# Decoder layer with product-key experts: the transposes of a key tile spread among the products of the tile before

## What is computed

```python
q = (ht @ w_q).reshape(t, PEER_HEADS, 2, PEER_HALF)
sc = jnp.einsum("thcd,hckd->thck", q, subkeys)
s1, i1 = lax.top_k(sc[:, :, 0], PEER_TOPK); s2, i2 = lax.top_k(sc[:, :, 1], PEER_TOPK)
...
experts = (e1 * PEER_N_KEYS + e2).reshape(t, PEER_HEADS * PEER_TOPK)
ug = jnp.take(u, eb, axis=0); vg = jnp.take(v, eb, axis=0)
act = jax.nn.gelu(jnp.einsum("tkd,td->tk", ug, hb)) * gb
return jnp.einsum("tk,tkd->td", act, vg)
```

## Time and profile before

| | |
|---|---|
| runs | 2933.47, 2937.51, 2937.99 us; median 2937.51 us |
| profiled execution | 2933.1 us, span of its instructions 2931.0 us |
| granted TensorE clock, mean | 0.995 |
| share of the span busy | TensorE matmuls 98%, weight loads 87%, VectorE 82%, GpSimd 57%, ScalarE 36% |
| the sweep | about 855 to 2183 us of the span |

### The profile page before, as it was taken

The page is one execution under the profiler, slowest core; times in us unless marked ns, Lnnn a source line. Parts: engine busy times, 40 slices in busy tenths (PEclk is TensorE's granted clock), DMA queues, the critical chain, the costliest instruction groups (busy, mean ns, idle before and its releaser), DMA issues.

```text
span 2931.0 us, 40438 instructions
## 1 busy us (share of the span) xinstructions
PE 2879.4 (98%) x14769; PEld 2546.0 (87%) x14769; DVE 2392.2 (82%) x3106; ACT 1057.1 (36%) x1375; POOL 1672.4 (57%) x1078
## 2 busy tenths in 40 slices
PE   7999999999999999999999999999999999999999
PEld 6888777778899999999999999999997777877787
DVE  6555888855679898988989898899777998999898
ACT  4121433341334343434333343444233333333333
POOL 1000565500116778765766666576868888887762
PEclk9999999999999999999999999999999999999999
DMA  8998999979978998999999999999999999999999
GB/s 300 328 354 275 307 307 297 302 277 335 308 261 304 328 355 307 347 322 342 335 314 348 310 341 329 332 341 365 335 367 394 411 419 416 418 421 419 419 416 375
DMA packets 332718, 1010.00 MB, mean 345 GB/s; under 512 B 65748, under 2 KB 182496, under 8 KB 247072
## 3 DMA queue, kind: packets, MB, share of 16 engines
q1 hardware_dynamic: 181648, 523.28, 48.0%
q0 software_dynamic: 113344, 454.44, 42.8%
q10 hardware_dynamic: 37584, 30.43, 3.2%
HBM read 881.01 MB, written 127.01 MB: 344 GB/s over the span
## 4 chain that ended last, share of the span: by engine, by line
PE 68%; DVE 11%; issue 6%; DMA 6%; POOL 6%; ACT 1%; ACTq 0%; DVEq 0%; SPq 0%; POOLq 0%
PE ps L2026 21%; PE ps L2028 21%; PE ps L2027 21%; POOL dots L975 4%; DMA v_ring<-in_peer_v,experts 4%; DVE x_rows L1871 2%; PE ps L2267 2%; POOL v_ring L986 2%; DVE x_one L1974 2%; DMA v_two<-in_peer_v 1%; DVE v_lo L1925 1%; DVE uT_lo L1835 1%; DVE u_row L1862 1%; PE ps L2109 1%; DMA wc_raw<-in_w_in 1%
## 5 line engine op out<-in xcount | busy, mean ns | idle before, releaser
L2026 PE MATMUL ps<-hT_hi,uT_hi 128*128 128x384 f32 x2048 | 697.3, 340 | 5.2 <-DVE uT_lo L1830 2.3
L2028 PE MATMUL ps<-h2T_lo,uT_hi 128*128 128x384 f32 x2048 | 686.0, 335 | 0.0
L2027 PE MATMUL ps<-hT_hi,uT_lo 128*128 128x384 f32 x2048 | 685.0, 334 | 0.0
L967 POOL DMA_INDIRECT grid<-gates,grid_cells x256 | 547.6, 2139 | 81.9 <-issue 81.9
L2026 PE MATMUL ps<-v_hi,a_hi 128*128 128x512 f32 x1024 | 407.4, 398 | 23.1 <-DVE v_lo L1925 22.3
L2027 PE MATMUL ps<-v_hi,a_lo 128*128 128x512 f32 x1024 | 404.8, 395 | 0.0
L2028 PE MATMUL ps<-v_lo,a_hi 128*128 128x512 f32 x1024 | 404.8, 395 | 0.0
L1342 ACT ACTIVATE v_hi<-v_two 128x2048 fp32r<-128x2048 f32 x126 | 241.6, 1918 | 447.4 <-PE ps L2028 376.0
L2026 PEld LDWEIGHTS ps<-hT_hi,uT_hi 128*128 128x128 f32 x2048 | 384.6, 188 | 17.3 <-DVE uT_lo L1835 6.5
L2027 PEld LDWEIGHTS ps<-hT_hi,uT_lo 128*128 128x128 f32 x2048 | 384.8, 188 | 1.9
L2028 PEld LDWEIGHTS ps<-h2T_lo,uT_hi 128*128 128x128 f32 x2048 | 384.3, 188 | 0.0
(11 more groups left out here) (210 smaller groups left out, 4957.0 us busy)
## 6 DMA issues: line engine op xcount, KB each, us to landing
v_two<-in_peer_v SPq DMA_DIRECT2D x63, 2048.0 KB
u_tile<-uT_all SPq DMA_DIRECT2D x70, 1024.0 KB
u_tile<-in_peer_u SPq DMA_DIRECT2D x58, 1024.0 KB
grid_rows<-grid SPq DMA_DIRECT2D x32, 1024.0 KB
half_rows<-in_peer_u SPq DMA_DIRECT2D x58, 512.0 KB, 7.2
uT_all<-half_turned POOLq DMA_DIRECT2D x232, 128.0 KB, 5.0
near_rows<-in_peer_u SPq DMA_DIRECT2D x25, 1024.0 KB, 8.2
uT_all<-near_turned SPq DMA_DIRECT2D x100, 256.0 KB, 7.0
```

The costliest lines, as they stand in the source:

```text
L967: pool.indirect_dma_start(out=grid, out_offset=bass.IndirectOffsetOnAxis(ap=grid_cells[:, d, col:col + 1], axis=0), in_=gates[:, 2 + d, co ...
L2026: mm(out, a_hi, b_hi, start=first, stop=False)
L2027: mm(out, a_lo, b_hi, start=False, stop=False)
L2028: return mm(out, a_hi, b_lo, start=False, stop=last)
```

## The change

Each transpose of the half is issued behind one group of three products, as `turned_amid(c + 1, half, k)` after the products of block k, instead of all eight after the 24. The wait for the load of tile c + 1 moves with the first transpose of the first half: it now comes after three products. `swept` is still set by the last product, which now has seven transposes ahead of it instead of none; the last transpose still sets `uT_half0_ps` or `uT_half1_ps`. The `turned` calls for tile 0 ahead of the sweep stay.

```diff
+            def turned_amid(c, half, k):
+
+                buffer = c % 2
+                if half == 0 and k == 0:
+                    pe.wait_ge(u_tile_in[buffer], 16 * (c // 2 + 1))
+                turning = turn(ps_uT[half][:, k, :], u_tile[buffer][:, (8 * half + k) * P:(8 * half + k + 1) * P],
+                               ident[:, :])
+                if k == 7:
+                    turning.then_inc(uT_half0_ps if half == 0 else uT_half1_ps[buffer], 1)
+
             def sweep(i, querying, last=False):
                 for b in range(TOPK):
                     c = TOPK * i + b
                     more = not (last and b == TOPK - 1)
-                    nxt = (b + 1) % 2
+                    turning = more and not turned_before(c + 1)
                     for half in range(2):
...
                                                     half == 0 and k == 0, half == 1 and k == 7)
-                        if half == 1:
-                            summed.then_inc(swept[b % 2], 1)
-                        if more and not turned_before(c + 1):
-                            turned(nxt, TOPK // 2 * i + (b + 1) // 2 + 1, half)
-                        elif more and half == 0:
+                            if half == 1 and k == 7:
+                                summed.then_inc(swept[b % 2], 1)
+                            if turning:
+                                turned_amid(c + 1, half, k)
+                        if more and not turning and half == 0:
                             summed.then_inc(uT_half0_ps, 1)
```

## The result

The changed kernel takes 2960.47 us in the median of four runs (2957.66 to 2965.96); the kernel before, run beside it, 2935.89. The ratio is 1.0087 (95% interval 1.0075 to 1.0099): 24.6 us slower, where +28.6 was forecast. The profiled execution is one of 2957.66 us.

A forecast was written before the change was run, and what follows sets the result against it. TensorE's in-order queue was taken to bound the sweep, busy for 1327.8 of 1333 us. The terms 2.4 + 29.2 - 6 + 3 = +28.6 us gave 2964 us, with a range of 2945 to 2985.

The forecast's parts named there:

- The transposes themselves: TensorE's sweep: 798 added changes from transpose to product at 0.003 us each, +2.4 us, ends 0 and +5.
- Faster: Rival: lone transposes between products hide in TensorE's stream, 0.052 us saved each, 47 us in all, 2917 us; chance 0.04.
- Much slower: Rival: each lone transpose on TensorE lays a weight load bare, about 0.109 us per change, 87 us, 3051 us; chance 0.06.
- The late loads: TensorE's moved wait, after 3 products instead of 24: loads late by 26.7 us plus 2.5 us of pipeline restarts, +29 us.
- the price of a load: Time of a tile's load from issue to landing, taken as 8.2 us, with 7.6 and 9.2 as ends.
- late by 6 x 2.5: First tiles of heads 1 to 6: windows of 5.7 us from issue to due, each load late by 2.5 us.
- eleven windows of 8.7 us: Tiles 18, 34, 50, 66, 82, 98 and 104 to 112 by twos: loads late by 0.3 us each, 3.3 us.
- the reading of the queues: Tile 126: from the DMA queues' moved bytes, the load lands at about 2157.4 and TensorE stands some 2.1 us.
- Absorption: TensorE's sweep: added time that falls where it was going to wait for VectorE anyway, taken as -6 us.
- The later `swept`: `swept` 0.76 us later delays ScalarE's second high part, felt at first tiles of 6 heads: +3 us, ends 0 and 4.6.
- The loads are in time: Rival: TensorE's moved wait finds the loads landed, at under 5.6 us each; only +2.4 to +7, 2942 us; chance 0.08.
- What would show it: Signs: TensorE waits for `u_tile` 15 to 21 times, 20 to 30 us; `uT_lo` waits hardly grow; VectorE's L1270 waits grow.

The follow-up runs named there:

- Experiment 1: Kernel before, transposes still in blocks of eight, only the wait for the next tile's load moved to after three products: 2950.87 us against 2936.48, ratio 1.0053.
- the first half alone: Changed kernel with only the first half's transposes one by one, the second half's again a block behind its 24 products: 2955.66 us, ratio 1.0065 to the kernel before.
- Experiment 3: Kernel before with the second half's transpose block ahead of its 24 products, SyncE also waiting for `swept` before its next load: 2946.45 us against 2936.48, ratio 1.0036.
- experiment 6: ScalarE's second high part put ahead of its two DMA issues: 2942.91 us on the changed kernel, 2935.28 on the kernel before, against 2935.76 for the kernel before.

## Why the prediction held, point by point

The time, the sign and the main mechanism held: the moved wait is the largest part. That the total came so close is luck, as all four terms were off, in both directions.

- *The transposes themselves, +2.4 us: small as forecast, mis-sized by nearly two.* A lone transpose takes 0.11 us, as in a block. The product behind it takes 3.5 ns longer than others and the product ahead 2.6: 4 to 5 us over 798 changes, at the forecast's upper end, where I had 0.003 us for a change. Both rivals on this point fall. Faster, by transposes that vanish in the stream: their steps are as long as in a block. Much slower, by exposed weight loads: 87 us would be 109 ns at each change, and there are some 6. The rule of the Trainium skill (TensorE: Matmul & The Clock Gate, Part 3, "The mechanism"), that only a load for another row group overlaps a running matmul, doesn't hold for these shapes; the same section also lets a load for the background weight buffer go ahead, which the prediction left out and which would fit.
- *The late loads, +29 us: the right mechanism, mis-sized by about two.* Experiment 1 shows +14.4 net; in the change the loads took 14.4 us of TensorE's time, restarts included, against 16.5 and 19.6 in the kernels with the wait alone and the first half alone. The step that failed is the price of a load, 8.2 us, taken from other tensors and set beside one late load. At the first tile of a head the waited-for loads took 6.5 to 7.4 us, so "late by 6 x 2.5" became 0.6 to 1.6 us each in five heads, 5.3 us in all, and nothing at tiles 64, 113 and 127. Of the eleven windows of 8.7 us eight became 9.4 to 9.5, as TensorE's own waits lengthen the tile, and the other three gave 0.8 us in two stalls instead of 3.3. Tile 126 alone was as long as in the sum, 3.5 us for 3.4 (the reading of the queues had given 2.1). The sum also had no term for the half clock behind that stall, 1.5 us.
- *Absorption, -6 us: mis-sized by about two.* The kernels with late loads and an early `swept` show -3.1 and -4.2 us, by the table. In the change it can't be seen by itself, as the later `swept` works against it, and together the two are +3.2 us where the forecast had -6 + 3 = -3.
- *The later `swept`, +3 us: mis-sized by three when alone.* Experiment 3 shows +10.0. I counted one tile in each of six heads and let up to 0.76 us pass on, 4.6 us; heads 0 to 5 of experiment 3 do show 4.6. What I had at nothing is heads 6 and 7. The late low part delays VectorE's whole queue, and the first half of the next tile waits too: head 6 grew by 2.8 us there and by 3.0 in the change. Head 7 grew by 3.4, behind a gather. The earlier trace rows held the sign of the main path: two issues of 0.33 and 0.63 us between Gelu and high part, which leave the high part no slack. I used it for one tile of a head and took the slack of the others from TensorE's, not from ScalarE's queue. In the change, where head 7 grew by 6.1 us, tile 126's stall and its half clock are 5 of them.
- *The loads are in time, 2942 us.* Refuted by ten waits of 12.0 us. The estimate by the Trainium skill (DMA: Bandwidth & Descriptors, "Anatomy of one DMA"), 4.4 us for such a load, lies under every load that was waited for; the shortest took 6.5. The section does not say how busy the engines were in its fit; here they were busy for 93% of the sweep. Two loads that nothing waited for were in within 5.7 us, so 4.4 is not excluded for those.
- *What would show it.* Waits for the load were to be 15 to 21, of 20 to 30 us: they are 10, of 12.0 us (15.1 on the weight loads), and longest at tile 126. VectorE's waits for L1270 grew as said, 35.8 to 65.0 us. That waits for `uT_lo` must not grow much was wrong. And one sign of being wrong came by the letter: products behind a transpose are longer, though by 3.5 ns and not by a weight load.

The sum by the change's own execution: loads 14.4, half clock 1.5, late halves +3.2, stream +4.3, together 23.4 us in the sweep. The forecast had 29, nothing, -3 and +2.4. About 13 us too much for the loads was made good by what the other terms lacked.

## What to carry to other kernels

In an in-order queue the place of a wait is a cost of its own: count what stands ready behind it, and read the window from the DMA's issue to that place for the shortest tiles, not for the mean one. Then follow each signal that comes later through the queue of the engine it releases: here 0.8 us of a late `swept` passed two DMA issues on ScalarE, a high part and VectorE's queue, and the kernel with that alone is 10 us slower. Issues that nobody waits for soon belong behind the work that the bound engine needs; that alone, in heads 0 to 6, made the kernel before faster, by 6.2 us, with no transpose moved.

## What was not expected of the hardware

A stop of TensorE can cost more than its length. After, TensorE's busy time and granted clock (the column behind POOL's) in two stretches at tile 126, the first with the stop of 3.52 us:

```profile
2172.50:2176.20 3.70, 0.18 (x2) 0.06 (x2) 2.81 (x3) 1.58 (x4) 3.09 (x3) 1.00 1.04 383
2176.50:2179.60 3.10, 3.10 (x13) 2.81 (x12) 2.21 (x1) 0.00 (x0) 1.19 (x2) 0.50 1.07 415
```

The clock is granted at 0.50 (1.2 GHz) for 3.4 us behind the stop, and then again at 1.00, with 27 matmuls in the 4.0 us from 2180.00. After, TensorE's timeline there:

```profile
2176.51 0.52 PE L2027 MATMUL ps<-hT_hi,uT_lo 128*128 128x384 f32 x1
2176.83 0.52 PE L2028 MATMUL ps<-h2T_lo,uT_hi 128*128 128x384 f32 x1
```

They end at 2177.03 and 2177.35: a step of 0.32 us instead of 0.173. Some ten products in that stretch make 1.5 us on top of the stall. The stalls of 1.8 us and less in this kernel show no such stretch, but the length alone doesn't decide. With the first half alone (experiment 2), two stops end at 1190.48 (2.57 us) and at 2175.08 (2.98 us); TensorE's rows behind each:

```profile
1190.60:1193.60 3.00, 3.00 (x12) 2.81 (x13) 2.97 (x4) 0.00 (x0) 2.20 (x2) 0.54 1.06 383
...
2175.30:2178.40 3.10, 3.10 (x22) 2.93 (x21) 2.27 (x2) 0.00 (x0) 0.90 (x2) 1.00 0.93 262
```

12 matmuls in 3.0 us behind the shorter stop, 22 in 3.1 behind the longer one. The wait alone (experiment 1) has the half clock behind a stop of only 1.82 us that ended at 931.40:

```profile
932.00:935.20 3.20, 3.20 (x12) 3.20 (x11) 3.10 (x6) 0.00 (x0) 2.90 (x2) 0.50 0.91 330
```

The change has 1.79 us at the same tile and stays at 1.00, and the change with experiment 6's edit stays at 1.00 behind a stop of 2.87 us. What decides between them was not tried. The twelve profiled sweeps hold none, one or two such stretches, so a difference of 1.5 us between single profiles means little.
